# A PEER mixer whose first row fetches, unit loads and masks are placed differently

## The reference

```python
def peer(h, peer_wq, peer_keys, peer_u, peer_v):
    ...
        sv, si = lax.top_k(s, PEER_TOPK)
        ...
        eid = jnp.take_along_axis(cid.reshape(PEER_BLOCK, PEER_HEADS, -1), ci, axis=-1)
        gate = jax.nn.softmax(cv, axis=-1).reshape(PEER_BLOCK, -1)
        ...
        u = jnp.take(peer_u, eid, axis=0)
        vv = jnp.take(peer_v, eid, axis=0)
        a = jax.nn.gelu(jnp.einsum('td,ted->te', xb, u).astype(jnp.float32), approximate=False) * gate
        return jnp.einsum('te,ted->td', a.astype(xb.dtype), vv)
```

## Time and profile before

| what | before |
|---|---|
| median of 3 runs | 3832.94 us (3831.51 to 3834.32) |
| the profiled execution | 3827.14 us, its span 3825.3 us, mean granted clock 0.921 |
| PE busy | 3269.1 us (85%) |
| DVE busy | 2488.0 us (65%) |
| POOL busy | 1708.6 us (45%) |
| ACT busy | 1089.1 us (28%) |
| gate stage | 1599.2 to 1753.0 us of the span |
| expert stage | 1753.0 to 3812.3 us |

### The profile page before, as it was taken

How to read it: one execution, slowest core, us unless ns; L and a number is a source line. 1 busy time by engine, 2 the same in 40 slices (tenths; PEclk the granted TensorE clock), 3 DMA queues, 4 the chain that set the end, 5 groups by cost and what they waited for, 6 DMA issues and landing times. The chain is left out here.

```text
span 3825.3 us, 46662 instructions
## 1 busy us (share of the span) xinstructions
PE 3269.1 (85%) x16946; PEld 2487.6 (65%) x16946; DVE 2488.0 (65%) x5652; ACT 1089.1 (28%) x2113; POOL 1708.6 (45%) x1354
## 2 busy tenths in 40 slices
PE   5999678999984988495788998999999999899987
PEld 4888567778773877494555666666666666566654
DVE  3000277767732799995977777777777777777743
ACT  3111234434422111293122222222222222222221
POOL 1000000000001244395777776777777776777753
PEclk7999789999996988697899999999999999999999
DMA  5222301111113100188999999999999999999987
GB/s 146 86 85 84 133 27 56 43 37 48 38 37 106 34 28 17 37 250 304 336 386 408 388 394 379 409 389 401 387 383 409 380 402 388 402 395 387 391 316 261
DMA packets 301121, 916.71 MB, mean 240 GB/s; under 512 B 27574, under 2 KB 111470, under 8 KB 283260
## 3 DMA queue, kind: packets, MB, share of 16 engines
q0 software_dynamic: 168048, 612.53, 41.4%
q1 hardware_dynamic: 132876, 301.61, 22.3%
HBM read 850.93 MB, written 64.32 MB: 239 GB/s over the span
## 5 line engine op out<-in xcount | busy, mean ns | idle before, releaser
L1143 POOL DMA_INDIRECT ex_row_u<-in_u_rows,eid_u x570 | 695.1, 1219 | 361.3 <-DVE ex_dots L1218 243.7
L1152 POOL DMA_INDIRECT ex_row_v<-in_v_rows,eid_v x576 | 727.5, 1263 | 265.7 <-issue 158.7
L1218 DVE CUSTOM_DVE_ANT_0 ex_row_u<-ex_row_u,ex_h2n 128x1024 f32<-128x1024 f32 x576 | 704.0, 1226 | 23.9 <-DMA ex_row_u<-in_u_rows,eid_u 23.8
L1329 PE MATMUL ex_psum_v<-ex_a_hi,ex_v_hi 128*128 128x512 f32 x1024 | 427.3, 417 | 122.3 <-DVE ex_y L1271 105.3
L395 POOL DMA_DIRECT2D rt_w_raw<-in_wq x2 | 1.1, 536 | 1112.3 <-POOLq L1542 1112.3
L1271 DVE TENSOR_TENSOR ex_y<-ex_y,ex_psum_v 128x512 f32<-128x512 f32 x504 | 340.3, 684 | 205.6 <-PE ex_psum_v L1329 205.4
L1313 PE MATMUL ex_psum_u<-h2d_hi,ex_u_hi 128*128 128x512 f32 x1024 | 410.9, 401 | 25.0 <-PEq L831 15.7
L1297 PE MATMUL ex_psum_g<-ex_row_v,ex_mask 128*32 128x512 f32 x2304 | 331.5, 701 | 111.5 <-ACT ex_mask L1182 92.5
L1329 PE MATMUL ex_psum_v<-ex_a_lo,ex_v_hi 128*128 128x512 f32 x1024 | 414.2, 404 | 0.0
L1329 PE MATMUL ex_psum_v<-ex_a_hi,ex_v_lo 128*128 128x512 f32 x1024 | 413.4, 404 | 0.0
L1313 PE MATMUL ex_psum_u<-h2d_lo,ex_u_hi 128*128 128x512 f32 x1024 | 402.9, 393 | 0.0
(11 more groups left out here) (323 smaller groups left out, 5711.8 us busy)
## 6 DMA issues: line engine op xcount, KB each, us to landing
ex_u_raw<-in_u SPq DMA_DIRECT2D x64, 1024.0 KB, 8.3
ex_v_raw<-in_v SPq DMA_DIRECT2D x64, 1024.0 KB, 7.9
gates<-gt_out SPq DMA_DIRECT2D x8, 4096.0 KB, 15.9
ex_gate<-gates SPq DMA_DIRECT2D x64, 512.0 KB, 6.8
mx_pj<-proj SPq DMA_DIRECT2D x9, 1796.0 KB, 7.2
proj<-pj_out SPq DMA_DIRECT2D x63, 225.0 KB, 2.0
pj_w_raw<-in_w_in SPq DMA_DIRECT2D x6, 1800.0 KB, 7.6
ex_row_u<-in_u_rows,eid_u POOLq DMA_INDIRECT x576, 8.6
```

What stands on the lines that cost most here:

```text
L1143: nc.gpsimd.indirect_dma_start(row_u[:, r % UR, :], None, u_rows, bass.IndirectOffsetOnAxis(eid_u[:, r:r + 1], 0)).then_inc(u_row[r % UR], 16)
L1152: nc.gpsimd.indirect_dma_start(row_v[:, r % VR, :], None, v_rows, bass.IndirectOffsetOnAxis(eid_v[:, V_TOK[r]:V_TOK[r] + 1], 0)).then_inc( ...
L1218: nc.vector.tensor_tensor_reduce(row_u[:, r % UR, :], row_u[:, r % UR, :], h2n[:, n % 2, :], 1.0, 0.0, ALU.mult, ALU.add, dots[:, n % 2, r ...
L1329: last = nc.tensor.matmul(psum_v[:, i % VB, :], a[:, j, d * P:(d + 1) * P], b[:, (s - 1) % 2, j, :], start=(m == 0), stop=(m == 3 * JG - 1))
```

## The change

Three edits.

1. In the gate stage POOL's loop over the blocks is written out, and the six first fetches are issued one behind each of the blocks 0 to 5 instead of all behind block 7.
2. A unit's 64 rows of `h2n` are loaded once, to partitions 0 to 63 (two DMAs less in the gate stage, seven less in the expert stage), and DVE copies them to partitions 64 to 127 ahead of the unit's first dot, with a wait for the copy behind it (nine copies and nine waits).
3. In `Timetable` the masks of a quad are put at the last ACT place ahead of the quad's place less 0.25 of a step. No other piece moves.

```diff
@@ gate_matrices
             for n in range(2):
-                for half in range(2):
-                    sp.dma_start(ahead.h2n[half * DEC:half * DEC + DEC, n, :], h2_units[n]).then_inc(ahead.h2_loaded[n], 16)
+                sp.dma_start(ahead.h2n[0:DEC, n, :], h2_units[n]).then_inc(ahead.h2_loaded[n], 16)
...
-            body(0, True)
-            with pool.Fori(1, NB) as b:
-                body(b, False)
-            for r in range(UR):
-                nc.gpsimd.indirect_dma_start(ahead.row_u[:, r, :], None, u_rows,
-                                             bass.IndirectOffsetOnAxis(eid_u[:, r:r + 1], 0)).then_inc(ahead.u_row[r], 16)
+
+            for b in range(NB):
+                body(b, b == 0)
+                if b < UR:
+                    nc.gpsimd.indirect_dma_start(
+                        ahead.row_u[:, b, :], None, u_rows,
+                        bass.IndirectOffsetOnAxis(eid_u[:, b:b + 1], 0)).then_inc(ahead.u_row[b], 16)
@@ Timetable.__init__
                 now = self.put("pe", self.quads, due, k)
-                self.put("act", self.masks, now, k, before=True)
+                self.put("act", self.masks, now - 0.25, k, before=True)
@@ experts
+        h2_doubled = sem("h2_doubled")
...
                 def load_h2(n):
-                    for half in range(2):
-                        sp.dma_start(h2n[half * DEC:half * DEC + DEC, n % 2, :],
-                                     h2_units[n]).then_inc(h2_loaded[n % 2], 16)
+                    sp.dma_start(h2n[0:DEC, n % 2, :], h2_units[n]).then_inc(h2_loaded[n % 2], 16)
...
                     if r % DEC == 0:
-                        dve.wait_ge(h2_loaded[n % 2], 32 * (n // 2 + 1))
+                        dve.wait_ge(h2_loaded[n % 2], 16 * (n // 2 + 1))
+                        nc.vector.tensor_copy(h2n[DEC:P, n % 2, :], h2n[0:DEC, n % 2, :]).then_inc(h2_doubled, 1)
+                        dve.wait_ge(h2_doubled, n + 1)
```

## The result

Five runs of each on one chip: 3832.94 us (3827.4 to 3835.03) for the kernel before, 3769.68 us (3762.34 to 3775.11) for the changed one. The ratio is 0.9837, 95% interval 0.9824 to 0.985. The forecast was 3774, so 59 us less; measured were 63 less.

| stretch | before | after | difference | forecast |
|---|---|---|---|---|
| start to gate stage (the change does not touch it) | 1599.2 | 1606.8 | +7.6 | 0 |
| gate stage to step 8 | 424.2 | 423.0 | -1.2 | 0 |
| steps 8 to 60 | 1616.7 | 1563.6 | -53.2 | -54, and most of the +3 for the copies |
| step 60 to the end | 185.2 | 174.6 | -10.6 | -8 |

A forecast was written before the change was run, and what follows sets the result against it. PE's chain was taken to set the pace, with DMA queues full behind it. Terms: -54 (steps 8 to 60), +3 (copies), 0 (first fetches), -8 (last steps), sum -59 from 3832.9: 3774 us, range 3740 to 3806.

The forecast's parts named there:

- M step: Expert-stage step with its quad at 0.44, 26 between steps 8 and 60; PE idled 2.92 us for a mask.
- Masks at 0.44: M steps: masks hidden behind `v_hi`, PE idles 1.10 instead of 2.92, plus 0.81 of clock; 26 times, 68 us saved.
- E: The moment in a step when PE has finished the second `psum_u` and ACT starts its Gelu.
- Masks at 0.68: Y steps: masks move ahead of `u_hi`, `u_lo` starts 0.54 us later, PE's wait 3.03 becomes 3.57; 14 us lost.
- Y steps: Expert-stage steps with the quad at 0.68, 26 between steps 8 and 60; PE idled 3.03 us for DVE's addition into `y`.
- The rival that the DMA is full: Engines cannot exceed 394 GB/s as a mean, so PE waits for rows instead; gain 13 us, 3820 us; chance 0.11.
- Rows of `h2n` loaded once: Expert stage: 1.8 MB less loading taken as 0; nine DVE copies with waits cost 3 us, ends 0 and 15.
- First fetches: Gate stage: last quad 3.3 us later, store's shared load 2.7 us less; taken as 0, ends -6 and +6.
- The clock came back: Rival denying this: the 1.10 us wait lowers PE's clock as long ones do; 3795 us; chance 0.12.
- the second rival: The clock gives all: 1.62 us in every M step, gain cut to 71 by the DMA's floor; 3757 us; chance 0.10.
- Late rows: Rival: late fetches hold DVE's dots, `u_lo`, `y` and PE; at 2 us per step +45, 3878 us; chance 0.05.
- the signs: Wrong if dots or quads wait for rows, M-step waits stay above 2 us, or Y-step waits grow over 0.5.

The follow-up runs named there:

- e4: The changed kernel without the third edit: first fetches between blocks and h2n rows loaded once, masks where they were before; 3830.97 us, ratio 0.9994 to the kernel before.
- e3: The kernel before with only the masks of the quads at 0.68 moved 0.25 of a step earlier; 3851.1 us, ratio 1.005.
- e2: The changed kernel, but with the masks of the quads at 0.68 left behind `u_hi` as before; 3747.65 us, ratio 0.9781 to the kernel before.
- e5: The changed kernel with masks at 0.68 left behind `u_hi`, and DVE's first two additions into `y` ahead of `u_lo`; 3737.25 us, ratio 0.9759 to the kernel before.
- e1: The kernel before with the third edit alone, all masks 0.25 of a step earlier; 3773.28 us, ratio 0.985.
- e8: The kernel before with masks moved earlier except those at 0.68, without the first two edits; 3756.81 us, ratio 0.9802.
- e6: The changed kernel with masks at 0.68 left behind `u_hi`, loading one of eight gate-matrix blocks after the first group; 3738.42 us, ratio 0.9753 to the kernel before.

## Why the prediction was right

**What bounds the kernel.** Held. The mask was what PE lacked: with it gone, the wait in an M step is 0.92 (e4 keeps the old one, and the old time).

**Masks at 0.44.** The mechanism held: the mask is hidden where ACT waits anyway, and `y` is next, at E + 7.08 (forecast E + 7.07). The term was 68 and came to 79. The idle part was sized about right: the three M steps of before in which no matmul was slow (13, 21 and 41) take 28.95, and 22 of the 26 of the changed kernel 27.2 to 27.4, so 1.74 was saved at an equal clock and not 1.82. The clock's part was sized too low. 0.81 was the mean of steps 21 and 22, but 23 of the 26 M steps were like step 22 (30.5 or more), and the mean M step lay 1.51 above those three. In the changed kernel the clock stays up in all 26. Steps 10, 17, 33 and 53 are longer for other reasons, 0.21 on the mean: 1.74 + 1.51 - 0.21 = 3.04.

**Masks at 0.68.** The mechanism held: 3.03 became 3.57 as forecast, and e3 shows the loss by itself. The size was wrong: 0.54 each, 14 us, left the clock out. The Y steps lost 1.00 each, 26 us. Before, four of them (27, 35, 47 and 55, of 31.4 instead of 33.0) had kept the clock behind their wait; in the changed kernel and in e3 none does, which is 1.6 each, some 6 us. e3's 0.77 is these two parts, 0.54 and 0.25. In four steps of the changed kernel (20, 23, 56 and 59) the lower level also lasted longer, 1.0 to 1.2 us each, and step 35, which waited for two rows, is 1.9 us longer. This error and the one at 0.44 cancel: 79 - 26 = 53, where 68 - 14 = 54 was forecast. So the nearness of the sum is partly luck, and the price hidden in it is the larger finding: e2, which leaves these masks where they were, is 16 to 22 us faster.

**The DMA.** Held for this kernel: the forecast said 408 GB/s and inside the limit, narrowly; 405 were moved and 4 us waited for rows. The rival that the DMA is full is not this kernel, but it is the next one: e2 touches it, e5 stands on it. The limit that the runs show is the 411 to 412 GB/s of the best slices; e5's slices over the same 1600 us:

```profile
GB/s 410 411 411 402 412 411 411 411 403 402 413 410 411 404 410 411 412 409 412 403 411 409 411 411 407 406 411 412 406 410 399 407 411 411 407 411 411 411 411 371
```

The Trainium skill (Perfetto Trace Analysis, Roofline) says that one core alone can go above the 358 GB/s share and is bounded by its 16 engines at about 435; the traces agree with the first, and no slice of 40 us that was read here came above 413.

**Rows of `h2n` loaded once.** The copy measured 0.69, between the bounds of 0.29 and 1.15, and the first dot starts 0.72 after it, so the wait behind it costs 0.03:

```profile
1781.24 0.69 DVE L1215 COPY ex_h2n<-ex_h2n 64x1024 f32<-64x1024 f32 x1
...
1781.96 1.23 DVE L1219 CUSTOM_DVE_ANT_0 ex_row_u<-ex_row_u,ex_h2n 128x1024 f32<-128x1024 f32 x1
```

Of the +3 some 2.3 can be found. In steps 10 and 17 a copy (of units 2 and 3) stands between E and `u_lo`, as foreseen, and PE waits 2.02 for `y`; in e1, which has no copies, it waits 1.19 and 1.38. In step 53 PE waits 1.22 for DVE's dots, and in e1 it does not. These steps are 0.84, 0.62 and 0.86 longer than in e1. Step 10, first in the changed kernel, then in e1:

```profile
2109.53 0.50 PE L1330 MATMUL ex_psum_v<-ex_a_hi,ex_v_hi 128*128 128x512 f32 x1 [2.02 <-DVE ex_y L1272]
...
2107.35 0.50 PE L1329 MATMUL ex_psum_v<-ex_a_hi,ex_v_hi 128*128 128x512 f32 x1 [1.19 <-DVE ex_y L1271]
```

e4 bounds both edits together to between -7 and +2 us. That the removed bytes count 0 was right as long as PE's chain set the pace, and probably wrong behind it (e8 against e2).

**First fetches.** The last quad ends 140.8 us after the stage's start instead of 137.2, 3.6 later (forecast 3.3). The load of the gate matrix is issued 159.4 us after it instead of 161.8:

```profile
1606.77 0.34 SPq L865 DMA_DIRECT2D ex_u_raw<-in_u  x1
...
1753.76 9.93 SPq L1105 DMA_DIRECT2D ex_u_raw<-in_u  x1
...
1766.15 0.33 SPq L1109 DMA_DIRECT2D ex_gate<-gates  x1
```

2.4 earlier, inside the 6 that the forecast allowed. The last store of the gate stage is issued 3.6 later too (at 1749.53), but the load follows it by 16.6 instead of 22.7, 6.0 less, where the forecast had put 2.7.

**Last steps.** -10.6 for -8. From 3540 on no matmul waits for a mask any more (one weight load does, 2.1); five did from 3600 on the earlier trace rows.

**The other rivals.** The clock came back, in the M steps in full (0.97 over the stretch; quads at 1.92). By the second rival they would be 1.82 + 1.62 = 3.44 shorter, and they are 3.04 shorter: three of them had not lost the clock before, and four are longer for other reasons. Late rows did not turn the sign in any kernel here, not even in e5 with 149 us of such waits, though its steps became irregular. Two of the signs that the prediction had named for being wrong did appear: the two waits for rows, 4 us in all, and a wait in the Y steps that grew by more than 0.5. The second contradicted the forecast itself, which had 3.03 become 3.57.

## What to carry to other kernels

Ask of a table edit what stands behind each moved instruction on its queue, place by place: here one line moved masks at three places, and one of them gained, one lost, and the third, at 0.22, which was not tried alone, shows no effect (e6's Y steps are as long as before); splitting it gave another 16 to 22 us. A wait that returns with each step costs more than its idle time if the engine's clock falls behind it, so a term for the clock belongs on both signs of the sum. When a resource reads as always busy, compute its floor from its best slices: it tells how far the next two edits can go, and which edits that are worth nothing today will count then.

## What the runs showed of the hardware

The longer PE's wait was, the oftener its clock was at the lower level behind it. After 0.91 or 0.92 it was so in none of the 23 M steps of the changed kernel (matmuls 0.40, quad 1.92); after 2.0 in none of its three, but in one of e6 (step 17, first matmul 0.80); after 2.9 and more in 23 of the 26 M steps before, and after 3.03 in 22 of the 26 Y steps (in e4, with the same waits, in 21 and 24); after 3.57 in all 26. In most of these steps it cost about 1.6 us (28.95 against 30.56 in M steps, 31.4 against 33.0 in Y steps).

The end of the gate stage was not expected as it came. Before, the first DMA of the expert stage is issued 7.4 us after POOL's last fetch has been issued (1745.61 to 1753.04). With the fetches out long before, it is issued 0.3 us after DVE's last work:

```profile
1751.20 2.29 DVE L904 TENSOR_TENSOR ex_u_lo<-ex_u_raw,ex_u_hi 128x2048 fp32r<-128x2048 f32 x1 [4.86 <-ACT ex_u_hi L969]
```

(1753.49 to 1753.76). That the stage's end waits until the fetches have landed fits both, and was not tried by itself.
